# Two transformer blocks on one core: conditional passes announced to the instruction fetch, and attention values one step later

## The chip, the cores and the metric

The kernel runs on one core of a Trainium2 chip. The metric is the device time of one execution in microseconds (us); the figure of a kernel is the median of several executions. Engines are named as in the profile: PE (TensorE, matmuls), PEld (its weight loads), DVE (VectorE), ACT (ScalarE), POOL (GpSimd), SP (SyncE, which issues the weight transfers). "PEq" and "PEldq" are PE's sequencer: semaphore events, register loads and branches.

## What is computed

256 tokens of width 1024 go through two blocks in float32. Each block is a mixer with three branches and then a mixture of experts:

```python
def first_block(x, ...):
    h = rms_norm(x, norm_mix) * (1 + sc_m) + sh_m
    x = x + g_m * hybrid_mixer(h, ...)          # linear recurrence, two attentions
    h = rms_norm(x, norm_ffn) * (1 + sc_f) + sh_f
    return x + g_f * moe_ffn(h, ...)            # 32 experts, top 4, w1 1024x2048, w2 1024x1024

def second_block(x, mem, ...):
    y_ssm = s5_branch(u_ssm, ...)               # complex state space, scans along the sequence
    y_dsa = dsa_branch(q, k, v, ...)            # 8 heads, top 64 keys of each query
    y_mem = memory_branch(qm, km, vm)           # 4 heads over 256 memory rows
    merged = g_s * (y_ssm @ w_up_ssm) + g_d * (y_dsa @ w_up_dsa) + g_m * (y_mem @ w_up_mem)
    x = x + merged @ w_out
    return x + hier_moe(rms_norm(x), ...)       # 32 experts in 4 groups, top 2
```

## The kernel before, in words

Each engine has its own instruction stream, written out by hand in one order; they meet at semaphores. `Queue` (L65) wraps an engine with the semaphore it raises, so `t(ins)` marks an instruction and returns its number, and the tables `pe`, `act` and `dve` hold these marks for the others to wait on. The program is written twice, once dry to fill the tables.

**First mixture** (`tensor_moe1`, L824). The weights of expert u are six transfers of 2 MB, w1 in four and w2 in two, 192 in all, which SP issues in order into eight slots of `ring` (`fetcher`, L303; `sync`, L325). A slot is filled again when PE has passed the marks that free it. The rows of an expert are gathered in groups of 32, up to four passes. The first pass is always computed. The others lie in the code behind the first and run only when a register with the expert's row count says so. This happens in three places for each expert: after either half of layer one, and after layer two's first pass. In each place the code of passes two to four comes first, and the short part that stands for "not more than 32 rows" comes after it, so a small expert jumps forward over all of the code of passes two to four. In a pass one half of layer one has 16 matmuls (32 rows x 512 columns, plus four for the bias in half one), and so has all of layer two. The helpers are `only` (L737) and `either` (L745); the places are L929 (`either(t, x, count, 32, second)`, twice per expert) and L961 to L973 (the If of the second pass of layer two and its Else). In the trace L748 is the condition of `either`, L755 the event that its Else raises, L962 the condition of the second pass of layer two, L970 and L973 the events of its Else. After either half, PE goes on with `spread1` of the expert before (L835; in the trace matmuls of L481), with the gather of the next expert and with layer two. The core of `either` is:

```python
with t.e.If(count > limit):
    body()
with t.e.Else():
    t.e.wait_ge(x.sem, m)
    t.e.nop().then_inc(x.sem, x.n - m)
```

**Second attention** (`tensor_dense2`, L981; `scalar_dense2`, L2442; DVE's loop behind L2022). Twelve units u = 0 to 11 (0 to 3 memory heads, 4 to 11 sparse heads) go through a pipeline of steps s. Per step PE does `scores(s)` (L1046, or L1049 and L1053), `turn_p(s-2)` (L609, transposes of the weights, in the trace L613) and `values(s-2)` (L1062 or L1067), with half a gate projection (L596) between them in steps 0 to 2. DVE does the row maximum of s (L1534, L1536), the scaling of the weights of s-1 (L1547, L1549) and one step of the state-space scan of group 0 (L2012 in steps 2 to 9, of 256 columns; other lines of 1024 columns in the first two and last four steps). ACT copies the result of values(s-3) out (L2520 or L2523), copies the turned weights of s-2 out of PSUM (`scalar_turned_p`, L2255; in the trace L2259) and takes the exponentials of s (`scalar_exps`, L2242; in the trace L2247). The turned weights lie in `PT[u % 2]`, two buffers; their PSUM bank (lane 6) and that of the values (lane 7) are single; `scalar_turned_p` of u waits for PE's values of u-2. After the loop PE does `driven(1)` (L1027), the input of the scan of group 1, and DVE the scans of groups 1, 2 and 3 (`scans`, L2022), each followed by `states` on PE (L1081; in the trace L488). Transfers for what follows wait for PE's mark of the last values (`pv`, 2, 11).

**Second mixture** (L1138 onward): 96 transfers of 2 MB in ten slots, no branches.

Of the kernel before, what the change touches and what calls it, by code (L numbers as in the profile page):

```python
# [64 lines left out]
class Queue:  # L65

    def __init__(self, e, sem):
        self.e, self.sem, self.n, self.met = e, sem, 0, {}

    def wait_ge(self, sem, value):
        if self.met.get(id(sem), 0) < value:
# [39 lines left out]
def build(nc, a, out, ctx):  # L112
# [632 lines left out]
    def either(t, x, count, limit, body):  # L745
# [6 lines left out]
        with t.e.Else():  # L752
            if m > 0:
                t.e.wait_ge(x.sem, m)
            t.e.nop().then_inc(x.sem, x.n - m)  # L755

    def tensor_rows(t, w, tb):

        for g in range(2):
            b = w.claim("rows", 1, tb, g)  # L760
            for i in range(4):
                ins = t.e.transpose(b[:, TB(i)], HV[:, 4 * g + i, TB(tb)], ident)
            pe["rows", 1, tb, g] = t(ins)
# [60 lines left out]
    def tensor_moe1(t, w):  # L824
        e = t.e
        tensor_route(t, w, 1, WR1, 32, 128)
        gather_rows(t, w, 1, 0, TL1)
        gather_weights(t, w, 1, 0, TL1)
        tensor_ada(t, w, 5, 1)
        t.wait_ge(s_dve, dve["flag", 1])  # L830
        t.wait_ge(s_b1, 16)

        x, y, z = Queue(e, s_px), Queue(e, s_py), Queue(e, s_ps)

        def spread1(u, count):  # L835
            spread(t, w, 1, u, TL1)

            def second_half():
                t.wait_ge(s_act, act["yg", 1, u, 1])
                for tb in range(2):  # L840
                    for h in range(2):
                        b = w.claim("sp", 1, u, 1, tb, h, lane=TL1X)
                        psp[u, tb, h] = z(e.matmul(b[:, :], SWT[u % 2][:, 1, TB(tb)], YG_[1][:, HALF(h)], start=True,
                                                   stop=True))

            either(t, z, count, 64, second_half)
            psp["all", u] = z.n

        def biases():

            for h in range(2):
                tensor_ada_out(t, w, 5, h, TL1)
            b = w.claim("ct", lane=TL1)
            for tb in range(2):
                ins = e.transpose(b[0:32, TB(tb)], CMB[:, tb, :], ident)
            pe["ct"] = t(ins)
            t.wait_ge(s_dve, dve["ct"])
            t.wait_ge(s_b2, 16)
            for tb in range(2):
                for h in range(2):  # L860
                    b = w.claim("y0", tb, h, lane=TL1)
                    pe["y0", tb, h] = w.sums(b[:, :], [(CT[:, TB(tb)], B2[:, HALF(h)])])

        counts = [e.value_load(flag(0))]
        for u in range(NE):
            HG, AT_ = HGB[u % 2], ATB[u % 2]
            pick = ident[0:32, u:u + 1].to_broadcast([32, 32])
            t.wait_ge(s_act, act["hg", 1, u])

            def layer1(b, n, half, arrive):  # L870

                if half == 0:
                    for s in range(4):
                        e.matmul(b[32 * s:32 * s + 32, :], pick, B1R[:, HALF(s)], start=True, stop=False)  # L874
                for c in (2 * half, 2 * half + 1):
                    if arrive:
                        w.weights("w1", u, c)
                    W = RG_(slot["w1", u, c], 0, 2, 2048)
                    for r in range(2):
                        for s in range(4):  # L880
                            ins = e.matmul(b[32 * s:32 * s + 32, :], HG[:, 2 * c + r, 32 * n:32 * n + 32],  # L881
                                           W[:, r, HALF(s)], start=False, stop=(c == 3 and r == 1))
                return ins

            def layer2(b, n, arrive, first):

                for s in range(4):
                    if arrive and s % 2 == 0:
                        w.weights("w2", u, s // 2)
                    W = RG_(slot["w2", u, s // 2], 0, 2, 2, 1024)  # L890
                    for h in range(2):
                        for r in range(2):
                            ins = e.matmul(b[64 * h + 32 * r:64 * h + 32 * r + 32, :],  # L893
                                           AT_[:, 2 * s + r, 32 * n:32 * n + 32], W[:, s % 2, r, HALF(h)],
                                           start=(s == 0), stop=(s == 3))
                            if first is not None:
                                first(ins)
                                first = None
                return ins

            def turn_act(k, passes):
                b = w.claim("at", u, k, lane=TL1)
                t.wait_ge(s_dve, dve["ac", u, passes[-1]])
                for i, n in enumerate(passes):
                    for r in range(2):
                        ins = e.transpose(b[:, TB(2 * i + r)], ACB[:, n, TB(r)], ident)  # L906
                return ins

            count = counts[u]
            b0 = w.claim("l1", u, 0, lane=(0,))  # L910
            for half in range(2):
                pe["l1", u, half] = t(layer1(b0, 0, half, True))
                if half == 1 and u + 1 < NE:
                    counts.append(e.value_load(flag(u + 1)))

                def further(n):
                    if half == 0:
                        w.claim("l1", u, n, lane=(n,))
                    return layer1(ps("l1", u, n), n, half, False)

                def third():
                    only(t, count, 96, lambda: further(3))
                    further(2)

                def second():
                    only(t, count, 64, third)
                    x(further(1))

                either(t, x, count, 32, second)  # L929
                for c in (2 * half, 2 * half + 1):  # L930
                    w.free("w1", u, c)
                    px["free", "w1", u, c], py["free", "w1", u, c] = x.n, 0
            px["l1", u] = x.n
            if u > 0:
                spread1(u - 1, counts[u - 1])
            if u == LATE_BIAS:
                biases()
            pe["at", u, 0] = t(turn_act(0, (0,)))
            if u + 1 < NE:
                gather(t, w, 1, u + 1, TL1)  # L940
            turn_act(1, (1,))
            t.wait_ge(s_act, act["at", u, 0])

            def first_second(ins):
                pe["at", u, 1] = t(ins)

            def first_third(ins):
                px["at", u, 2] = x(ins)

            pe["l2", u, 0] = t(layer2(w.claim("l2", u, 0, lane=(7,)), 0, True, first_second))  # L950

            def fourth():
                layer2(w.claim("l2", u, 3, lane=(3,)), 3, False, None)

            def third():
                t.wait_ge(s_act, act["at", u, 2])
                only(t, count, 96, fourth)
                y(layer2(w.claim("l2", u, 2, lane=(2,)), 2, False, None))

            m, met = (x.n, y.n), dict(t.met)  # L961
            with e.If(count > 32):  # L962
                only(t, count, 64, lambda: turn_act(2, (2, 3)))
                t.wait_ge(s_act, act["at", u, 1])
                x(layer2(w.claim("l2", u, 1, lane=(1,)), 1, False, first_third))
                either(t, y, count, 64, third)
            t.met = met
            with e.Else():
                t.e.wait_ge(s_px, m[0])
                e.nop().then_inc(s_px, x.n - m[0])  # L970
                if m[1] > 0:
                    t.e.wait_ge(s_py, m[1])
                e.nop().then_inc(s_py, y.n - m[1])  # L973
            px["l2", u] = x.n
            py["l2", u] = y.n
            for g in range(2):
                w.free("w2", u, g)
                px["free", "w2", u, g], py["free", "w2", u, g] = x.n, y.n
        spread1(NE - 1, counts[NE - 1])

    def tensor_dense2(t, w):  # L981
# [86 lines left out]
                                       start=(c == 0), stop=(c == 1))  # L1068
            pe["pv", 2, u] = t(ins)

        for s in range(14):
            if s < 12:
                scores(s)
            if s >= 2:
                turn_p(t, w, 2, s - 2, (0, 1), 2)
            if s < 3:
                gate_half(t, w, 2, 11 + s)
            if s >= 2:
                values(s - 2)

        def states(c):  # L1081
            WR_, WM_, TA_, TB_ = W5[c % 2]
# [1359 lines left out]
    def scalar_dense2(s):  # L2442
# [84 lines left out]
            if u == 11:  # L2527
                act["branch", 2, 1] = k

        for k in range(14):  # L2530
            if k >= 3:
                values(k - 3)
            if k >= 2:
                scalar_turned_p(s, 2, k - 2, 4)
            if k < 12:
                scalar_exps(s, 2, k, 256, 128.0 ** -0.5 if k < 4 else 0.125, False)
# [170 lines left out]
```

## Time and profile before

| | us |
|---|---|
| median of 3 executions | 2187.61 |
| lowest and highest | 2186.37, 2188.66 |
| the profiled execution | 2187.02 |
| its span, first to last instruction | 2185.2 |
| PE busy | 1818.3 |
| DVE busy | 804.7 |
| ACT busy | 506.8 |
| read from HBM | 709.35 MB |

The span is what the rows further down are counted in (their times run from its start); the profiled execution's own time has 1.8 us more around it. PE's busy time is modelled and the matmuls overlap, so its share says little by itself: what counts is which wait ends last in each stretch.

### The profile page before, as it was taken

Reading aid. Unit: us, or ns where it says so; the run is one execution under the profiler, and the core shown is the slowest. Engines: PE = TensorE matmul, PEld = TensorE weight load, DVE = VectorE, ACT = ScalarE, POOL = GpSimd, SP = SyncE. Lnnn points to the kernel's source line nnn. Section 1 sums busy time; section 2 is a strip of 40 time slices with the busy share of each in tenths; the row PEclk is TensorE's granted clock in tenths of the full one; section 3 lists DMA queues with packets and bytes.
Section 4 is the critical chain, followed back from the end, with each engine's and each line's share of the span. In section 5 each row is a group of like instructions: output and inputs, shape, how many; then the busy total and the mean of one; then the engine's idle time right before and its main releaser. Section 6 shows DMA issues by size and latency. Waiting matters only on the chain. (4 is left out here: it accounts for less than half of the span.)

```text
span 2185.2 us, 28329 instructions
## 1 busy us (share of the span) xinstructions
PE 1818.3 (83%) x11496; PEld 826.7 (38%) x11496; DVE 804.7 (37%) x1613; ACT 506.8 (23%) x1028; POOL 77.5 (4%) x96
## 2 busy tenths in 40 slices
PE   7899998999999998989987797699889855665556
PEld 3655445433333433424333233255544522222221
DVE  2215533333342444434443334588782200000001
ACT  2022302232331233332333233222310200000000
POOL 0000000000000000000000000084000000000000
PEclk9999999999999999989999999799999878887888
DMA  7845359789897799999999999534128299999997
GB/s 281 287 136 191 136 173 388 314 350 409 343 420 312 309 424 423 423 422 399 425 423 423 422 423 423 180 121 178 54 101 345 87 429 427 427 428 428 427 429 322
DMA packets 114820, 713.55 MB, mean 327 GB/s; under 512 B 16799, under 2 KB 21102, under 8 KB 69006
## 3 DMA queue, kind: packets, MB, share of 16 engines
q1 hardware_dynamic: 106208, 704.98, 79.1%
q10 hardware_dynamic: 8398, 5.47, 0.8%
q8 instruction: 165, 2.70, 0.5%
q14 instruction: 49, 0.40, 0.0%
HBM read 709.35 MB, written 1.07 MB: 325 GB/s over the span
## 5 line engine op out<-in xcount | busy, mean ns | idle before, releaser
L881 PE MATMUL ps<-ring,ar 128*32 128x512 f32 x3072 | 371.9, 624 | 44.3 <-DMA ring<-in_w 31.6
L481 PE MATMUL ps<-ar 128*128 128x128 f32 (+5 forms) x1742 | 351.4, 359 | 38.3 <-PEq L755 16.4
L488 PE MATMUL ps<-ring,ar 128*32 128x512 f32 x1184 | 196.1, 692 | 139.0 <-DMA ring<-in_w_gate 49.2
L481 PEld LDWEIGHTS ps<-ar 128*128 128x128 f32 (+2 forms) x1742 | 233.9, 200 | 159.4 <-issue 114.3
L481 PE MATMUL ps<-ring,ar 128*128 128x512 f32 (+2 forms) x592 | 247.0, 577 | 4.9 <-ACT ar L2266 2.6
L881 PEld LDWEIGHTS ps<-ring,ar 128*32 128x32 f32 x3072 | 97.8, 113 | 314.3 <-issue 264.7
L1825 DVE TENSOR_SCALAR ar<-ps 128x256 f32<-128x256 f32 x128 | 54.4, 425 | 409.7 <-PE ps L881 400.9
L893 PE MATMUL ps<-ring,ar 128*32 128x512 f32 x1536 | 173.8, 598 | 0.0
L596 PE MATMUL ps<-ring,ar 128*128 128x512 f32 x384 | 171.9, 599 | 0.0
L481 PEld LDWEIGHTS ps<-ring,ar 128*128 128x128 f32 x592 | 112.4, 191 | 132.8 <-issue 126.2
L2400 ACT ACTIVATE ar<-ps 64x512 f32<-64x512 f32 x256 | 151.5, 592 | 45.1 <-PE ps L893 30.7
L1748 DVE TENSOR_TENSOR ar<-ps,ar 128x512 f32<-128x512 f32 x176 | 121.7, 692 | 91.0 <-PE ps L481 80.7
L488 PEld LDWEIGHTS ps<-ring,ar 128*32 128x32 f32 x1184 | 54.9, 124 | 247.5 <-issue 246.7
L488 PE MATMUL ps<-ar 128*32 128x512 f32 x288 | 112.6, 701 | 36.8 <-DMA ring<-in_w_up 21.3
L2389 ACT ACTIVATE ar<-ar 128x256 f32<-128x256 f32 x128 | 53.3, 416 | 322.0 <-DVE ar L1825 316.0
L1835 DVE TENSOR_TENSOR ar<-ar 128x256 f32<-128x256 f32 x128 | 79.6, 622 | 97.2 <-ACT ar L2389 90.4
L2437 ACT ACTIVATE ar<-ps 128x256 f32<-128x256 f32 x128 | 49.2, 384 | 252.3 <-PE ps L906 203.5
L596 PEld LDWEIGHTS ps<-ring,ar 128*128 128x128 f32 x384 | 71.8, 192 | 80.9 <-issue 80.5
L2124 DVE TENSOR_TENSOR ar<-ps,ar 128x512 f32<-128x512 f32 x8 | 5.5, 692 | 263.1 <-ACT ar L2576 263.1
L893 PEld LDWEIGHTS ps<-ring,ar 128*32 128x32 f32 x1536 | 46.3, 110 | 100.4 <-issue 100.4
L2368 ACT ACTIVATE ar<-ps 128x512 f32<-128x512 f32 x80 | 47.8, 597 | 95.1 <-PE ps L481 95.1
L874 PE MATMUL ps<-ar 32*32 32x512 f32 x384 | 54.1, 619 | 14.4 <-PEq L973 10.3
(403 smaller groups left out, 1379.0 us busy)
## 6 DMA issues: line engine op xcount, KB each, us to landing
ring<-in_w SPq DMA_DIRECT2D x192, 2048.0 KB, 20.4
ring<-in_w_gate SPq DMA_DIRECT2D x25, 2048.0 KB, 29.1
ring<-in_w_up SPq DMA_DIRECT2D x25, 2048.0 KB, 31.4
ring<-in_w_down SPq DMA_DIRECT2D x24, 2048.0 KB, 29.8
ring<-in_w_in SPq DMA_DIRECT2D x21, 2048.0 KB, 9.0
ring<-in_w_ada SPq DMA_DIRECT2D x12, 2048.0 KB, 8.3
ar<-in_w_up SPq DMA_DIRECT2D x7, 2048.0 KB, 29.8
ar<-in_w_gate SPq DMA_DIRECT2D x7, 2048.0 KB, 29.3
```

The lines of the kernel that those rows point to most:

```text
L481: ins = self.t.e.matmul(o, l, r, start=(i == 0), stop=(i == len(pairs) - 1))
L488: ins = self.t.e.matmul(b[32 * i:32 * i + 32, :], l, r, start=(k == 0), stop=(k == len(steps) - 1))
L596: ins = t.e.matmul(b[:, :], HV[:, k, TB(tb)], W[:, k, :], start=(k == 0), stop=(k == 7))
L874: e.matmul(b[32 * s:32 * s + 32, :], pick, B1R[:, HALF(s)], start=True, stop=False)
L881: ins = e.matmul(b[32 * s:32 * s + 32, :], HG[:, 2 * c + r, 32 * n:32 * n + 32], W[:, r, HALF(s)], start=False, stop=(c == 3 and r == 1))
L893: ins = e.matmul(b[64 * h + 32 * r:64 * h + 32 * r + 32, :], AT_[:, 2 * s + r, 32 * n:32 * n + 32], W[:, s % 2, r, HALF(h)], start=(s == 0 ...
L1748: k = v(v.own.tensor_tensor(o, b, o, ALU.add))
L1825: dve["glu", u, n] = v(v.own.tensor_scalar(glu, b[:, 0:512:2], 7.0, None, ALU.min))
L1835: dve["ac", u, n] = v(v.own.tensor_tensor(o, lin.rearrange("p (q r) -> p q r", r=2), sg.rearrange("p (q r) -> p q r", r=2), ALU.mult))
L2389: act["sg", u, n] = s(s.own.activation(M[:, 512:768], M[:, 0:256], ACT.Sigmoid, scale=1.702))
L2400: k = s(s.own.activation(YG_[n // 2][64 * (n % 2):64 * (n % 2) + 64, HALF(h)], ps("l2", u, n)[64 * h:64 * h + 64, :], ACT.Copy))
L2437: m = s(s.own.activation(o, ps("at", u, k)[:, 256 * i:256 * i + 256].rearrange("p (r s n) -> p r s n", r=2, s=4), ACT.Copy))
```

## The change

Three edits.

There are three hints per expert: before the first half of layer one, right after the first branch for the second, right after the second for the branch in layer two.
2. The three places are rewritten with a new function `announced`, which writes the compare-and-branch and the two parts by hand: the branch is taken to "other" when the count is below 33, the body follows it. The nested conditions (64 and 96 rows) stay as they were, without hints.
3. In the second attention, `values` on PE goes from step s-2 to step s-3, with one step more at the end, and its copy on ACT from k-3 to k-4. `turn_p` and the copy of the turned weights stay where they were.

```diff
+    def announced(t, name, count, limit, notice, body, other):
+
+        e, met = t.e, dict(t.met)
+        part = lambda end: e if t.dry else nc.body(f"{name}_{end}", valid_engines=[e.engine])
+        e.br_lt(count, limit + 1, on_true=f"{name}_other", on_false=f"{name}_body").branch_hint(notice)
+        with part("body"):
+            body()
+            e.br(f"{name}_end")
+        t.met = met
+        with part("other"):
+            other()
+            e.br(f"{name}_end")
+        if not t.dry:
+            nc.switch_bb(f"{name}_end")
...
             count = counts[u]
+            more = e.to_reg(count > 32)
+            notice = e.mark_branch_hint_location(more)
             b0 = w.claim("l1", u, 0, lane=(0,))
...
-                either(t, x, count, 32, second)
+                m = x.n
+
+                def none():
+                    if m > 0:
+                        e.wait_ge(s_px, m)
+                    e.nop().then_inc(s_px, x.n - m)
+
+                announced(t, f"first{u}_{half}", count, 32, notice, second, none)
+                notice = e.mark_branch_hint_location(more)
...
-            with e.If(count > 32):
+            def second_pass():
                 only(t, count, 64, lambda: turn_act(2, (2, 3)))
...
-            with e.Else():
-                t.e.wait_ge(s_px, m[0])
+            def no_second_pass():
+                e.wait_ge(s_px, m[0])
...
+            announced(t, f"second{u}", count, 32, notice, second_pass, no_second_pass)
...
-        for s in range(14):
+        for s in range(15):
             if s < 12:
                 scores(s)
-            if s >= 2:
+            if 2 <= s < 14:
                 turn_p(t, w, 2, s - 2, (0, 1), 2)
             if s < 3:
                 gate_half(t, w, 2, 11 + s)
-            if s >= 2:
-                values(s - 2)
+            if s >= 3:
+                values(s - 3)
...
-        for k in range(14):
-            if k >= 3:
-                values(k - 3)
-            if k >= 2:
+        for k in range(15):
+            if k >= 4:
+                values(k - 4)
+            if 2 <= k < 14:
                 scalar_turned_p(s, 2, k - 2, 4)
```

## Rows read from the trace of the kernel before

**Rows 1.** The page, its first line.

```profile
span 2185.2 us, 28329 instructions
```

**Rows 2.** Engines by stretch: busy us (count) of each, PEclk, DMA share, GB/s.

```profile
392.00:745.00 353.00, 335.48 (x2632) 128.90 (x2628) 126.43 (x264) 97.41 (x191) 0.00 (x0) 0.99 0.87 355
...
936.00:1380.00 444.00, 382.51 (x2738) 149.89 (x2734) 173.91 (x360) 140.87 (x275) 0.00 (x0) 0.95 1.00 417
...
1568.00:1628.00 60.00, 54.44 (x228) 24.70 (x224) 56.62 (x69) 4.27 (x6) 0.00 (x0) 0.96 0.25 88
...
1752.00:2172.00 420.00, 241.64 (x1706) 94.50 (x1702) 37.70 (x55) 28.38 (x50) 0.00 (x0) 0.79 1.00 425
```

**Rows 3.** The same view, one short stretch of the first mixture.

```profile
723.00:745.00 22.00, 20.63 (x182) 9.07 (x184) 8.53 (x19) 9.32 (x18) 0.00 (x0) 1.00 0.41 157
```

**Rows 4.** Waits of PE, 392 to 745 us: total us, times, longest.

```profile
PE ps L481 <- PEq L755: 5.4, 3, 2.5
...
PE ps L881 <- PEq L755: 1.2, 2, 1.0
```

**Rows 5.** Waits of PE, 936 to 1380 us.

```profile
PE ps L881 <- DMA ring<-in_w: 31.6, 16, 3.1
```

**Rows 6.** Timeline of PE, 421 to 432 us: start, us, what, idle before and releaser.

```profile
431.34 1.43 PE L481 MATMUL ps<-ar 128*128 128x512 f32 x2 [2.49 <-PEq L755]
```

**Rows 7.** Branches and Else events by line, 392 to 745 us: ns min/median/max, first and last.

```profile
L748 PEldq COMPARE_BRANCH  x55: 65/179/4721, 393.6 to 742.8; - x55
...
L962 PEldq COMPARE_BRANCH  x10: 70/76/422, 413.5 to 729.3; - x10
...
L973 PEldq EVENT_SEMAPHORE  x4: 51/51/51, 443.2 to 644.7; - x4
```

**Rows 8.** The same view of line 748 alone from 426.4 to 426.5 us, and of line 1202.

```profile
L748 PEldq COMPARE_BRANCH  x1: 4721/4721/4721, 426.5 to 426.5; - x1
...
L1202 PEldq COMPARE_BRANCH  x1: 3761/3761/3761, 1392.9 to 1392.9; - x1
```

**Rows 9.** Timeline of the second attention, one step with sparse heads.

```profile
1546.29 0.69 DVE L1534 TENSOR_REDUCE small<-ps 128x2 f32<-128x512 f32 x1 [0.90 <-PE ps L1053]
1546.73 0.60 ACT L2259 ACTIVATE ar<-ps 128x512 f32<-128x512 f32 x1 [1.34 <-PE ps L613]
...
1547.47 0.66 PE L1067 MATMUL ps<-ar 128*64 128x128 f32 x8 [0.78 <-ACT ar L2259]
...
1548.06 0.70 PE L1049 MATMUL ps<-ar 64*128 64x256 f32 x4
1548.27 0.69 DVE L2012 TENSOR_TENSOR_SCAN ring<-ar,ring 128x256 f32<-128x256 f32 x1
...
1548.69 1.13 PE L1053 MATMUL ps<-ar 128*128 128x256 f32 x4
...
1549.66 0.60 PE L613 MATMUL ps<-ar 128*128 128x128 f32 x4
1549.86 0.69 DVE L1534 TENSOR_REDUCE small<-ps 128x2 f32<-128x512 f32 x1 [0.90 <-PE ps L1053]
```

**Rows 10.** The same timeline, earlier steps, with memory heads' values, and one later scan step.

```profile
1528.66 1.05 PE L1062 MATMUL ps<-ar 128*128 128x128 f32 x8
1529.55 1.03 PE L1046 MATMUL ps<-ar 128*128 128x256 f32 x4
...
1538.69 0.69 DVE L1534 TENSOR_REDUCE small<-ps 128x2 f32<-128x512 f32 x1 [1.37 <-PE ps L1053]
...
1542.73 0.69 DVE L1534 TENSOR_REDUCE small<-ps 128x2 f32<-128x512 f32 x1 [1.37 <-PE ps L1053]
...
1558.97 1.23 DVE L2014 SCALAR_TENSOR_TENSOR ring<-ring 128x1024 f32<-128x1024 f32 x1
```

**Rows 11.** Waits of PE, 1528 to 1567 us.

```profile
PE ps L1067 <- ACT ar L2259: 6.3, 8, 0.8
```

**Rows 12.** Timeline behind the last scan: PE's first matmul after the wait.

```profile
1628.20 1.08 PE L488 MATMUL ps<-ar,ring 128*32 128x256 f32 x8 [4.97 <-DVE ring L2039]
```

More of the change, by code:

```diff
@@ L69, in __init__ @@
         self.e, self.sem, self.n, self.met = e, sem, 0, {}
+        self.dry = isinstance(e, Dry)
     def wait_ge(self, sem, value):
@@ L958, in third @@
                 y(layer2(w.claim("l2", u, 2, lane=(2,)), 2, False, None))
-            m, met = (x.n, y.n), dict(t.met)
-            with e.If(count > 32):
+            m = (x.n, y.n)
+            def second_pass():
                 only(t, count, 64, lambda: turn_act(2, (2, 3)))
@@ L966, in tensor_moe1 @@
                 either(t, y, count, 64, third)
-            t.met = met
-            with e.Else():
-                t.e.wait_ge(s_px, m[0])
+            def no_second_pass():
+                e.wait_ge(s_px, m[0])
                 e.nop().then_inc(s_px, x.n - m[0])
                 if m[1] > 0:
-                    t.e.wait_ge(s_py, m[1])
+                    e.wait_ge(s_py, m[1])
                 e.nop().then_inc(s_py, y.n - m[1])
+            announced(t, f"second{u}", count, 32, notice, second_pass, no_second_pass)
             px["l2", u] = x.n
```

## The prediction, made before the changed kernel was run

> **What bounds the kernel now.** I read the stages first, then PE's waits within the two stretches that the change touches, then the timeline of one step. The profiled execution took 2187.02 us around a span of 2185.2 us [rows 1]; that is 0.59 us below the median shown, 2187.61. All sums below are made against 2187.02.
>
> The first mixture has two regimes. From 392 to 745 us the weight transfers run at 355 GB/s with a DMA share of 0.87, from 936 to 1380 us at 417 GB/s with a share of 1.00 [rows 2]. In the first regime SP stands still in places because no ring slot is free: from 723 to 745 us the share is 0.41 at 157 GB/s, while PE is busy for 20.63 of 22 us [rows 3], and PE's waits there name no weight transfer, only small things, among them the Else event L755 [rows 4]. PE is the bound, and a microsecond that it loses or saves before 745 us moves all later transfers. In the second regime PE waits for weights, 31.6 us in 16 waits [rows 5]: transfers are the bound, and what PE saves there is waited away at the next transfer.
>
> In the second attention PE, ACT and PE again form one chain per step: PE turns the weights of u (L613), ACT copies them (L2259), and PE, which can do nothing else in its order, waits 0.78 us and then does the values (L1067) [rows 9]. From 1568 to 1628 us DVE's scans bound (56.62 of 60 us busy [rows 2]); PE waits for the last of them, 4.97 us [rows 12]. The second mixture runs at 425 GB/s with a share of 1.00 [rows 2]; it begins with its slots full, so that what the dense part saves ahead of it comes off the end in full.
>
> **The change, part by part. Values a step later.** PE's step with sparse heads starts its pieces at 1547.47 (values), 1548.06 and 1548.69 (scores) and 1549.66 (transposes) [rows 9]. Values cost 0.59 to the next start, scores 0.63 and 0.97; each is 0.07 to 0.16 shorter than the row's own duration, since matmuls overlap, so the transposes, 0.60, count for 0.44 by my estimate (the larger of the two cuts). That is 2.63 us of PE's own work in a period of 1549.86 - 1546.29 = 3.57 us [rows 9]; the other 0.94 is the wait for ACT and the drain around it. After the change the values that stand behind the transposes are those of the unit before, whose copy ACT has made a step ago, and the wait goes. Next in line is DVE: its row maximum starts at 1546.29 and its scan step ends at 1548.27 + 0.69 = 1548.96 [rows 9], 2.67 us of work; with a start I take 2.70 per step. ACT's share of a step is smaller (0.60 for the copy, then exponentials and the copy of the values), and all that it now does later it does in time that it idled, 1.34 us a step [rows 9].
>
> With the memory heads' values the period is 1542.73 - 1538.69 = 4.04 us [rows 10]; less 0.94 it is 3.10, PE's own. Step by step, taking DVE's row maximum of step s as the clock: the first values leave step 2, so step 3 starts 1529.55 - 1528.66 = 0.89 us earlier [rows 10]. Steps 4, 5 and 6 take 3.10 for 4.04: 2.82. Step 7 took 3.57 and now has the last memory values: 3.10, so 0.47. Steps 8, 9 and 10 take 2.70 for 3.57: 2.61. Before step 11 DVE has a scan step of 1.23 in place of 0.69 [rows 9, 10], so 3.24 for 3.57: 0.33. The sum is 7.1 us. Behind the last row maximum both kernels have the same chain (scaling, scan steps, last transposes, ACT's copy, last values): the values of unit 10 lie beside ACT's last copy. `driven(1)` and DVE's scans start 7.1 us earlier. Price range: the profile puts PE's waits for ACT under L1067 at 6.3 us in 8 times [rows 11], of which DVE keeps some back, so at least 4; at most, if DVE's idle time went entirely, 0.90 for each of eight steps [rows 9] and 0.89, 8.1. The buffers hold: ACT writes a `PT` buffer after the values of u-2, which stand one step ahead of it in PE's order, so this adds no wait. What follows is bound by DVE and then by PE; its transfers are issued at the marks that move with it, and the DMA share in that stretch is 0.25 [rows 2].
>
> **Announced conditions.** What there is to win is in the branches. Of the 55 executions of L748 before 745 us the median is 179 ns and the longest 4721; the ten of L962 stay below 422 ns [rows 7]. A long one empties PE's queue: the branch at 426.5 us took 4.72 us [rows 8], and PE stood 2.49 us [rows 6]; the other 2.23 us were covered by matmuls queued already. Before 745 us such idle time adds up to 5.4 + 1.2 = 6.6 us in five waits [rows 4]; this is all that hints can give, since what is lost later is covered by waiting for transfers [rows 5]. I take 0. Most taken branches are short: four experts with at most 32 rows end before 745 us [rows 7], and none of their L962 branches took over 422 ns, though each jumps over three passes. So the target normally is at hand, and a long branch must be one that comes too soon after the fetch had last moved on. 
>
> The Trainium skill's page Runtime: NRT & Kernel Launch, section Instruction fetch mechanics, says that instructions come in blocks of 256, that only the next block is fetched ahead, and that a taken branch stalls if its target is in neither. By that rule no jump of 240 reaches beyond the next block, a hint has nothing to redirect, and yet 4.72 us should not occur; the trace disagrees on the last point, so it must be lateness of the next block. By the rule the sum is that of 0; if the hints cured every stall of the rows it would be 6.6 lower.
>
> The hints and the register cost some five short sequencer instructions per expert. A branch that finds its target costs 65 to 76 ns [rows 7], so I bound each by 0.1 us; PE works off its queue meanwhile (2.23 us of cover above), so 0. Without cover it would be 0.5 us for each of ten experts before 745 us, 5 us. They also shift all later code, so that other branches come too soon; which ones I can't tell from rows, and take the number as unchanged, from none (6.6 saved) to twice as many (6.6 lost).
>
> The sum: 2187.02 - 7.1 - 0 = 2179.9 us. I predict 2180.0.
>
> **The rivals.** *Hints cure the stalls.* If the fetch starts on the target when the hint executes, 80 instructions or a whole half ahead, the lateness is gone. For it: the stalls are of the size of a fetch made at need, as at L1202, 3.76 us [rows 8]. Against it: the target already is next. Time: 2187.0 - 7.1 - 6.6 = 2173.3.
>
> *Hints misdirect the fetch; the kernel becomes slower.* If a hint makes the fetch leave out the block that comes next, or fetch one that is there, each announced branch of a small expert, or the code just behind it, waits. Place: 14 announced and taken branches before 745 us (four experts with three, one with two). Price: 2.49 us each [rows 6], 34.9, less the 6.6 there are: 28.3 more, 2187.0 - 7.1 + 28.3 = 2208. It decides over the sign from 7.1 us on, half a microsecond per branch. For it: nothing in this profile; against it: a hint at 1 does nothing, and one at 0 names a block that is wanted.
>
> *Another engine takes over in the attention.* If ACT's queue (the copy of the values now comes ahead of the copy of the weights) or DVE's holds the step at 3.1 or 3.2 us, the gain is 3 to 4 us: 2183.5.
>
> *The stalls only move.* The shift alone makes more branches late, 3 to 6 us more: 2183 to 2186.
>
> **How the numbers follow.** Forecast 0.55; cure 0.20; misdirection 0.09; another engine 0.08; moved stalls 0.08. A measurement of this kernel tells about 0.2%, 4.4 us, from no change. Faster by more: forecast, cure and a third of the two small ones, 0.80. Within: 0.12. Slower: misdirection less its mild cases, 0.08. The range holds forecast and cure and reaches into the moved stalls: 2172.5 to 2184.5.
>
> **What would show it.** Right: the row maxima L1534 of steps 8 to 10 stand 2.70 us apart, PE has no wait for L2259 at L1067, DVE's idle before L1534 is near zero there; from L1534 of step 11 to the end of the span the distance is unchanged; PEq waits at L755 and its successor before 745 us sum to 3 to 10 us. Wrong: they vanish (cure), or long branches stand at nearly every small expert (misdirection). Also wrong: DVE's scans from 1560 us on don't start earlier, or the second mixture's transfers wait for something else.

## The result, and the profile after

The changed kernel takes 2198.14 us (median of six executions, 2192.04 to 2199.65); beside it the kernel before took 2187.43 (six, 2185.67 to 2190.69). The ratio is 1.0037, 95% interval 1.0024 to 1.005: it is slower, by about 8 us by the ratio and 10.7 between the two medians, where 7 us less had been forecast; the stated range ended at 2184.5. The profiled execution took 2198.91 us, 11.9 more than the one before. (One of the twelve executions of `values_again` further down took 3727.53 us, in the slow state, and is left out of its figures.)

The two halves of the change went opposite ways. Take DVE's first sum behind the first mixture (L1854 before, L1883 after) as the border: it starts at 1399.83 us before and at 1418.90 after, 19.1 us later; from there to the end of the span are 785.4 us before and 778.2 after, 7.2 less. So the loss lies in the first mixture.

The page of the kernel after (its first line), and its engines by stretch, with the columns of [rows 2]:

```profile
span 2197.1 us, 28459 instructions
```
```profile
392.00:745.00 353.00, 331.07 (x2634) 129.79 (x2636) 126.67 (x264) 96.42 (x188) 0.00 (x0) 0.99 0.86 352
745.00:936.00 191.00, 166.35 (x1138) 69.24 (x1134) 78.84 (x161) 61.58 (x120) 0.00 (x0) 0.92 0.98 410
936.00:1380.00 444.00, 387.59 (x2770) 159.34 (x2766) 179.94 (x374) 143.68 (x281) 0.00 (x0) 0.94 0.98 408
```

The middle stretch before had 423 GB/s; in the last, transfers ran at 417 GB/s before [rows 2] and run at 408 now. Worked out from these rates (the difference times the length of the stretch), the transfers fell behind by some 3, 6 and 10 us in the three stretches: an estimate, but it accounts for nearly all of the 19.1 us and puts all but 3 of it behind 745 us, where the forecast had counted on cover. The transfers no longer bound in the last stretch, as PE's waits between 936 and 1380 us show (total us, times, longest):

```profile
PE ps L922 <- PEq L756: 11.1, 2, 5.6
PE ps L890 <- ACT ar L2466: 11.0, 4, 2.9
PE ps L897 <- issue: 9.4, 4, 3.3
PE ps L482 <- PEq L952: 8.9, 7, 2.4
PE ps L897 <- PEq L952: 5.3, 2, 3.1
PE ps L890 <- issue: 3.2, 1, 3.2
PE ps L897 <- DMA ring<-in_w: 2.1, 2, 1.9
```

The 31.6 us of waiting for weights [rows 5] have shrunk to 2.1, and waits for PE's own sequencer stand in their place. L952 is the event behind the announced conditions of layer one, L756 that behind the condition "more than 64 rows" of `spread1`, which is not announced (its branch is L749); what comes late is the branch ahead of them. The four waits put down to ACT's L2466 each follow an announced branch of layer two that took 4.7 to 5.1 us, so they belong here too. All but the last line sum to 48.9 us; in the kernel before, the same view has 19.8 us of such waits (7.6, 5.3, 4.6, 2.0 and 0.3). The growth, 29.1, is about what the wait for weights lost, 29.5. One trace does not fix the 19.8, though: with the mixture's code as it was before, the traces of `values_only` and `values_again` have 29.3 and 34.0 us of such waits there, and 22.2 and 26.8 of waiting for weights. The new and largest item is that of L756, two waits of over 5 us that the kernel before did not have.

Before 745 us the same view answers to [rows 4]:

```profile
PE ps L482 <- PEq L952: 4.1, 3, 2.6
PE ps L859 <- issue: 2.7, 1, 2.7
PE ps L890 <- ACT ar L2466: 2.3, 1, 2.3
PE ps L897 <- issue: 1.7, 1, 1.7
PE ps L890 <- issue: 1.5, 1, 1.5
PE ps L897 <- PEq L952: 1.0, 1, 1.0
```

Idle time for the events of announced branches is 5.1 us where it was 6.6: little was cured. But "issue", idle time without a releaser, is 5.9 us where it was 2.0, and the line with ACT is again a late branch, 4.53 us at 593.7 us.

In the second attention the clock of the steps, DVE's row maximum (L1563, before L1534), answers to [rows 9] and [rows 10]:

```profile
1563.94 0.69 DVE L1563 TENSOR_REDUCE small<-ps 128x2 f32<-128x512 f32 x1
1565.92 0.69 DVE L2041 TENSOR_TENSOR_SCAN ring<-ar,ring 128x256 f32<-128x256 f32 x1
1566.72 0.69 DVE L1563 TENSOR_REDUCE small<-ps 128x2 f32<-128x512 f32 x1
...
1569.49 0.69 DVE L1563 TENSOR_REDUCE small<-ps 128x2 f32<-128x512 f32 x1
...
1572.80 0.69 DVE L1563 TENSOR_REDUCE small<-ps 128x2 f32<-128x512 f32 x1
```

The steps are 2.78, 2.77 and 3.31 us; the brackets with idle time before them are gone, so DVE is the bound of these three steps. PE's waits from 1547 to 1586 us are now these, with no wait for the copy of the weights [rows 11]:

```profile
PE ps L614 <- DVE ar L1578: 2.8, 2, 1.8
PE ps L1096 <- ACT ar L2552: 0.4, 1, 0.4
```

### The profile page after: what moved, and what is told of

The parts are those of the page before. It is cut to its first block and busy times, and to the rows that moved or that the text cites. A ratio compares the mean times of both kernels' runs of the same rounds, so it can differ in the third digit from the quotient of the medians.

```text
span 2197.1 us, 28459 instructions
## 1 busy us (share of the span) xinstructions
PE 1823.7 (83%) x11496; PEld 836.6 (38%) x11496; DVE 804.9 (37%) x1613; ACT 507.2 (23%) x1028; POOL 77.5 (4%) x96
## 5 line engine op out<-in xcount | busy, mean ns | idle before, releaser
L482 PE MATMUL ps<-ar 128*128 128x128 f32 (+5 forms) x1742 | 355.6, 362 | 37.7 <-PEq L952 17.0
L482 PEld LDWEIGHTS ps<-ar 128*128 128x128 f32 (+2 forms) x1742 | 237.9, 203 | 157.1 <-issue 112.2
L482 PE MATMUL ps<-ring,ar 128*128 128x512 f32 (+2 forms) x592 | 247.0, 577 | 3.8 <-DVE ar L1452 1.9
L1854 DVE TENSOR_SCALAR ar<-ps 128x256 f32<-128x256 f32 x128 | 54.4, 425 | 406.0 <-PE ps L897 397.1
L482 PEld LDWEIGHTS ps<-ring,ar 128*128 128x128 f32 x592 | 112.4, 191 | 131.9 <-issue 126.2
L2466 ACT ACTIVATE ar<-ps 128x256 f32<-128x256 f32 x128 | 49.2, 384 | 270.1 <-PE ps L922 219.8
```

The costliest lines, as they stand in the source:

```text
L482: ins = self.t.e.matmul(o, l, r, start=(i == 0), stop=(i == len(pairs) - 1))
L1854: dve["glu", u, n] = v(v.own.tensor_scalar(glu, b[:, 0:512:2], 7.0, None, ALU.min))
L2466: m = s(s.own.activation(o, ps("at", u, k)[:, 256 * i:256 * i + 256].rearrange("p (r s n) -> p r s n", r=2, s=4), ACT.Copy))
```

## The experiments

Two theories stood after reading the two traces. Shift: the four added instructions per expert (one for the register, three hints) move all branches in the code, and more of them come before their block is fetched. Hint: announcing a branch that will be taken spoils the fetch in certain places. The Trainium skill's page Runtime: NRT & Kernel Launch, section Instruction fetch mechanics, says that code comes in blocks of 256 instructions, 16 KiB, and that only the next one is fetched ahead. The trace agrees on the size: queue 8, whose packets follow PE's branches and so carry PE's code, moved 2.70 MB in 165 packets, 16 KB each. "Fetch" below is the start of such a packet.

```profile
q8 instruction: 165, 2.70, 0.5%
```

### The two parts alone

`values_only` and `values_again` are the same kernel, the one before with the third edit alone; `announced_only` is the one before with edits 1 and 2.

> Only the attention edit; the first mixture is as before. If the attention gives what the two profiles suggest (DVE's first scan behind the attention starts 4.6 to 5.5 us earlier, seen from the end of the mixture, and the rest is 2.6 us shorter), the time is 2187.4 - 7.2 = 2180.2; if only the 4.6 us count, 2182.8. Rival: the two edits work on each other, and the attention alone gives nothing: 2187.

> The attention edit alone once more, beside far_early on one chip: five kernels that share it and differ in the mixture's code alone stood at 2183 to 2184.6, this one at 2179.7. If the layout of the branches costs those 3 to 5 us: 2179 to 2181 again. If that was chance: 2182 to 2184.

> Only the announced conditions; the attention is as before. If the parts add up: after plus what the attention gives, 2198.1 + 7.2 = 2205.3, and the mixture's end stands 19 us behind that of before. If the loss comes from something that both edits make together: less than 2200.

The attention alone gave 2179.74 us (ratio to before 0.9958, 0.9943 to 0.9974) and, run again, 2183.38 (0.9971, 0.9957 to 0.9984): 6 to 9 us less by the ratios, as forecast. The second figure is where its expectation put chance, not a cost of the layout, as the reason why other kernels stood 3 to 5 us above the first. The conditions alone gave 2203.5 (1.0079, 1.0064 to 1.0094): 15 to 17 us more. The parts add up, 1.0079 - 0.0036 = 1.0043 against the 1.0037 measured.

### The same code positions without hints, and with hints that say "straight on"

`shift_four` has the old branches and, in place of the four new instructions, empty events; `straight` is the changed kernel with a register that is always 1.

```diff
+            for _ in range(2):
+                e.nop().then_inc(s_pad, 1)
...
                 either(t, x, count, 32, second)
+                e.nop().then_inc(s_pad, 1)
```
```diff
-            more = e.to_reg(count > 32)
+            more = e.to_reg(count > -1)
```

> Values later, the old branches, no hints, but four empty events of PE per expert at the places of the register instruction and the three hints, so that every block of 256 instructions holds what it holds in the changed kernel. Shift theory (the loss comes from where branches fall in the blocks): 2197 to 2200, with the long branches at the same places as in the changed kernel, except those that need a hint. Hint theory (the loss is the hints' own): 2180 to 2182. If both have a share, in between: two stalls of 6.5 us at L749 in the changed kernel, both in same-block jumps, should be gone.

> The changed kernel, but the hinted register is always 1, so that each hint says that the branch goes straight on, wrongly for small experts. Shift theory: a hint that says straight asks only for what is fetched anyway, so the time is that of the shift alone, 2197 to 2200. Theory that a taken hint with its target in the same block puts off the next block: the two stalls of 6.5 us at L749 go, 5 us or so less than after: 2192 to 2194. Theory that the hint helps at long jumps: slower than after, over 2200.

They took 2184.62 us (0.9989, 0.9976 to 1.0003) and 2183.8 (0.9986, 0.9973 to 0.9999). The shift theory as the main cause has fallen: with the same number of instructions in the same places the time stays below that of the changed kernel, by 10 to 11 us by the ratios and 14 by the medians. So has the thought that hint instructions cost much in themselves: they are all executed in `straight`. What costs is a hint that says "taken". Both times also lie above the 2180 to 2182 of the pure hint theory, so that the shift may have a share. In `straight` the two waits for L756 are gone and the waits for weights are back; PE from 936 to 1380 us:

```profile
PE ps L897 <- DMA ring<-in_w: 21.8, 11, 3.0
PE ps L890 <- ACT ar L2466: 12.0, 4, 3.3
PE ps L482 <- PEq L952: 6.4, 5, 1.8
PE ps L897 <- PEq L952: 4.4, 2, 3.1
PE ps L897 <- issue: 4.3, 2, 2.9
```

Behind the first line these are 27.1 us (28.2 with one more of 1.1 us), inside the 19.8 to 34.0 of the three traces with the old code; the 48.9 of after stands out.

### Which hints

Laying the code of the changed kernel beside its trace gives the position of each executed branch. 63 announced branches are taken (21 experts with at most 32 rows, three each). At five the target lies in the same block as the branch, by my estimate of where blocks begin; there the branch takes 0.23 us, and the next fetch comes late: 8.5, 10.9 and 10.6 us after it at the second halves of experts 3, 16 and 22, where `straight` has 3.8, 3.6 and 3.5, and 4.5 and 4.3 us at layer two of experts 19 and 25, where `straight` has 2.3 and 2.7. The 40 others up to expert 23's second half take what they take in `straight`, within 0.7 us. Behind that, nine of the 18 others differ by 1.1 to 4.3 us, some longer and some shorter; why was not followed, so there the two kernels are not alike in all but the five. The first of the five is expert 3's second half. Timeline of PE after:

```profile
508.06 1.88 PE L859 MATMUL ps<-ar 128*128 128x512 f32 x4
510.28 0.70 PE L859 MATMUL ps<-ar 128*128 128x512 f32 x1 [0.34 <-DVE ar L1777]
513.63 2.08 PE L859 MATMUL ps<-ar 128*128 128x512 f32 x2 [2.65 <-issue]
```

and in `straight`:

```profile
511.25 1.98 PE L859 MATMUL ps<-ar 128*128 128x512 f32 x4 [0.34 <-DVE ar L1777]
```

PE runs into the end of its code within one group of four matmuls. The next fetch starts 8.5 us after the branch there (511.14 against 502.66), in `straight` 3.8 us after it (507.41 against 503.62). The clock makes it worse in this trace. Engines by stretch after, with PEclk as the third column from the right:

```profile
506.00:510.00 4.00, 3.75 (x9) 1.14 (x7) 3.48 (x6) 0.00 (x0) 0.00 (x0) 1.00 1.05 446
510.00:513.00 3.00, 0.70 (x1) 0.19 (x1) 0.92 (x2) 0.00 (x0) 0.00 (x0) 0.91 1.00 415
514.00:518.00 4.00, 4.00 (x11) 2.34 (x11) 1.95 (x4) 0.51 (x2) 0.00 (x0) 0.50 1.01 424
518.00:522.00 4.00, 4.00 (x32) 3.98 (x30) 1.15 (x3) 1.49 (x3) 0.00 (x0) 0.84 1.00 420
```

and in `announced_only`, which has the same stall (2.4 us):

```profile
514.00:518.00 4.00, 4.00 (x32) 3.47 (x32) 2.66 (x5) 1.58 (x3) 0.00 (x0) 1.00 0.95 395
```

Behind the idle 2.65 us the granted clock is 0.50, the lower level of 1.2 GHz, for some 5 us. Two of the four matmuls take 2.08 us, where in `straight` all four take 1.98. From expert 3's second branch to expert 4's first the changed kernel needs 25.5 us, `announced_only` 22.4 and `straight` 19.8. So the late fetch cost 2.6 us here, and the dip of the clock 3.0 more; the same stall can come with it or without. The same distance at experts 16 and 22 is 25.6 and 25.3 us after, 19.1 and 18.7 in `straight`. Not all of this stays: counted from expert 0's first branch, the changed kernel is 24.1 us behind `straight` at expert 23's first and 16.3 behind at expert 31's second.

Two kernels test this, each with the changed kernel's positions. `hint_across` leaves out the five hints, `hint_within` has only these five (empty events in the places of the others).

```diff
+    SAME = {(3, 1), (16, 1), (22, 1), (19, 2), (25, 2)}
...
+            def hint(k):
+                if (u, k) not in SAME:
+                    return e.mark_branch_hint_location(more)
+                e.nop().then_inc(s_pad, 1)
```

> The changed kernel, but five of its 96 branches go without a hint (an empty event stands in place of the hint instruction): expert 3, 16 and 22 at the second half of layer one, expert 19 and 25 at layer two. By the spacing of the code fetches these are the taken branches whose target lies in the same block of 256 instructions as the branch itself. Theory that only such hints cost: the time of the kernel with four empty events, 2183 to 2186, and PE's stalls of 6.5 us at L749 are gone. Theory that every hint of a taken branch costs a little: near 2195. Theory that hints across a block boundary help: below 2180.

> The complement: only those five branches have a hint, the other 91 have an empty event in its place; every block holds what it holds in the changed kernel. Theory that only such hints cost: the time of the changed kernel, 2196 to 2200. Theory that the loss is spread over all hints: near 2184.

91 hints: 2184.13 us (0.9982, 0.9967 to 0.9997), as without any. Five hints: 2197.0 (1.0035, 1.002 to 1.0051), the time of the changed kernel. So these five are what makes it slower than the layouts beside it. The waits of `hint_across` from 936 to 1380 us, and then those of `hint_within`:

```profile
PE ps L901 <- DMA ring<-in_w: 23.6, 12, 3.1
```
```profile
PE ps L926 <- PEq L756: 10.2, 2, 5.2
...
PE ps L901 <- DMA ring<-in_w: 5.7, 3, 3.0
```

The transfer queues in the 8 us behind expert 3's second branch, in `hint_across` (499.8 to 507.9 us) and in `hint_within` (500.4 to 508.6), show the fetch that is missing; packets, MB, share:

```profile
q1 hardware_dynamic: 235, 3.46, 100.6%
q8 instruction: 1, 0.02, 0.7%
```
```profile
q1 hardware_dynamic: 235, 3.46, 99.0%
```

### Another place for all of the code

> Values later and the old branches, no hints; one never taken body of 200 empty events stands ahead of expert 0, so that all code of the mixture lies 201 instructions further on. Nothing else changes. Shift theory: a block is late when PE passes the one before it in less than 5.9 us; worked out for this layout from the times of the branches, stalls before 745 us grow by 7 us (sum 14.6 against 7.7) and those of the whole mixture by 10: 2187 to 2190. Theory that the place of the code doesn't matter: 2179.7 to 2180.5.

> The changed kernel with all its hints, and a never taken body of 60 events ahead of expert 0: all its branches lie 61 instructions further on, nothing else differs. Theory that a taken hint within one block of 256 stops the fetch of the next block: the five stalls of the changed kernel (experts 3, 16 and 22 at half two, 19 and 25 at layer two) go, and late fetches stand at 14 to 16 other branches, among them half two of experts 5, 10, 11, 17, 23, 24, 29 and 30 and layer two of experts 1, 7, 13, 15 and 26. At the 2.6 us that each of the five cost (hint_within against hint_across, 12.9 us), 14 to 16 of them cost 36 to 42, less what is hidden: 2205 to 2225. Rival, that only the number of hints or their instructions count, or something peculiar to those five experts: 2184 to 2200.

The padding is a body behind a condition that is never true, ahead of expert 0:

```diff
         counts = [e.value_load(flag(0))]
+        with e.If(counts[0] > 4096):
+            for _ in range(60):
+                e.nop().then_inc(s_pad, 1)
```

`pad_200` took 2183.8 us (0.9985, 0.997 to 1.0). That is some 4 us above `values_only` and 0.4 above `values_again`, between the ranges of both theories, and my working of the late blocks failed: before 745 us PE waited 1.1 us for L755, less than the 6.6 of [rows 4], not more. `after_pad_60` took 2205.76 (1.0065, 1.0041 to 1.009), with a median in the range expected of the hint theory; but its five executions go from 2194.09 to 2206.29, two of them in or near the rival's range. What tells the theories apart is the trace. The late fetches at the five old places are gone (their branches now take 0.6 to 5.0 us, as jumps into the next block do) and new ones are there: at expert 5's second half the announced branch is short, as a jump within a block is, and PE stands later without a releaser. L762 and the timeline of PE there:

```profile
L762 PEldq COMPARE_BRANCH  x1: 233/233/233, 575.5 to 575.5; - x1
```
```profile
583.12 1.99 PE L859 MATMUL ps<-ar 128*128 128x512 f32 x4 [0.34 <-DVE ar L1780]
589.94 0.44 PE L925 MATMUL ps<-ar 128*128 128x128 f32 x2 [4.84 <-issue]
```

The next fetch came 12 us after that branch, and 8.3, 9.8 and 8.1 us after those of experts 11, 24 and 30. But only six branches were of this kind, not 14 to 16: these four and layer two of experts 15 and 21 (0.24 and 0.23 us, next fetch 4.3 and 4.2 us later). The others that the expectation names took 3.2 to 5.0 us, so they did leave their block, and my block boundaries are off there. Five of the six are among those it names. At 2.6 us each, six come to 16 us, not to 36 to 42, so that the median fell into the range is partly luck. The branches behind new block starts have a share that is not known (six announced first halves take 6.0 to 6.5 us here); no kernel with this layout and without hints was run.

### Hints for a jump that is far

Behind the mixture PE, DVE and ACT branch over a region of thousands of instructions (L1202). PE's 3.76 us there [rows 8] hurt nobody, but DVE's stand on the chain that ended last. These kernels have the attention edit, the old branches in the mixture, and a hint for this one on PE and DVE.

```diff
-            self.cond = q.e.If(q.e.value_load(flag) > 0)
+                q.e.br_lt(value, 1, on_true=self.end, on_false=f"{name}_body").branch_hint(notice)
...
+            value = q.e.value_load(FLG[m - 1][0:1, 0:1].bitcast(I32))
+            notices[q.e.engine, m] = value, q.e.mark_branch_hint_location(q.e.to_reg(value > 0))
```

> Values later and the old branches, without hints in the mixture; but the branch of L1202 behind the mixture, which skips a region of thousands of instructions, is announced on PE and on DVE ahead of the last expert's spread. In the trace with the attention edit alone, PE's branch there takes 3.48 us and DVE stands 3.50 us behind its own, on the chain that ended last. Theory that a hint starts the fetch of its target: both shrink below 0.5 us and the time falls by 3.0, 2179.7 to 2176.7. Theory that a hint only stops the fetch of the next block: the same stall or a longer one, 2179.7 to 2183.

> As far_hint, but the hint for the far branch behind the mixture executes much earlier: on PE at the start of the last expert (some 900 instructions ahead), on DVE three experts ahead. In far_hint it executed 8.3 us ahead of PE's branch, but after PE had entered the block that holds the branch; PE still took 3.23 us there and DVE 2.80 us behind its own. Theory that the choice of the next block to fetch falls on entering a block, and that a hint turns it to the target: both branches fall below 0.6 us, DVE's chain is 2.8 us shorter, 2180 to 2177. Theory that hints do nothing at far targets either: the same 3 us on both, 2180 to 2184.

> far_early with a never taken body of 28 events ahead of expert 0, so that the mixture's code lies 29 instructions further on; the sum of late blocks worked out from the branch times would fall from 42 to 35 us over the whole mixture, but the same working failed for the shift by 201. If the layout is worth 3 to 5 us either way: between 2174 and 2182; if it is worth nothing that can be measured: as far_early.

With the hint late (`far_hint`: 2183.03 us, 0.9969, 0.9953 to 0.9985) both stalls stayed, 3.23 us on PE and 2.80 behind DVE's branch. With the hint early both went. The two kernels load and compare the value alike and differ only in when that and the hint execute: 8.2 us ahead of PE's branch in `far_hint`, 36.5 in `far_early`. That it is the entry into the block that decides, and not the time ahead, no run separates. DVE's first sum in `values_again`, then the same in `far_early`; the last line is PE's branch in `far_early`:

```profile
1403.61 1.23 DVE L1854 TENSOR_TENSOR ar<-ar 128x1024 f32<-128x1024 f32 x1 [3.36 <-issue]
```
```profile
1393.04 1.23 DVE L1880 TENSOR_TENSOR ar<-ar 128x1024 f32<-128x1024 f32 x1 [0.73 <-DVEq L1797]
...
L1210 PEldq COMPARE_BRANCH  x1: 444/444/444, 1388.5 to 1388.5; - x1
```

`far_early` took 2180.22 us (0.9976, 0.9962 to 0.9989) and `far_early_28` 2182.04 (0.9973, 0.996 to 0.9986). The stall fell by 2.6 us in the trace, but it did not come off the end. From DVE's first sum to the end of the span are 781.7 us in `far_early` and in `far_early_28`, 779.1 in `values_again`, 779.6 in `far_hint`. The difference lies behind the attention: from DVE's row maximum of step 11 to PE's first matmul behind the last scan are 70.2 us in these two and 67.9 in `values_again` and `far_hint`, and in these two the clock is 0.50 for 5 us around the start of `driven(1)`. Such a dip stands in `values_only` too, which has no hint, so that the early hint brings it on is not shown. These two, `far_hint` and the attention edit alone are faster than the kernel before by 0.2 to 0.4% and can't be told from each other.

## Why the prediction was wrong

**The term that failed** is the "- 0" for the announced conditions, a sum of nothing with bounds of 6.6 us either way. `announced_only` measured it at 15 to 17 us more. Two steps behind it were wrong, the second decisively.

**What bounds, and the cover behind 745 us.** The two regimes were read rightly, but the step "what is lost later is covered by waiting for transfers" failed. The cover was finite, 31.6 us [rows 5], and its use is in the rows: 2.1 us of it are left. The stretch was never summed. From 936 to 1380 us the waits for the sequencer went from 19.8 us (29.3 and 34.0 in the other two traces of that code) to 48.9, which used up what there was to hide, and four of the five harmful hints lie at 935.9 us or behind.

**Hints at 0.** This is the step that decided the sign. "A hint that names the target doesn't start that fetch earlier if it is already the next one due" held for the 58 branches whose target lies in the next block: together they cost nothing that can be told, 0.9982 in `hint_across` against 0.9989 and 0.9986 in `shift_four` and `straight`. It didn't ask about a target in the branch's own block. Its own numbers held the case: a jump of 192 instructions inside blocks of 256 stays in its block from up to a quarter of all positions (an estimate; three of the 21 second halves did, four in `after_pad_60`). In the five cases of this kind a fetch that would have been made was made late: `hint_within` against `hint_across` is 2197.0 - 2184.1 = 12.9 us (11.6 by the ratios), 2.6 per case on average, net of what later waits give back and with the lower clock in it. The rival "hints misdirect the fetch" had this mechanism, "make the fetch leave out the block that comes next", and got 0.09; its place and size were wrong. It charged 14 branches before 745 us (13 by the trace: expert 10's second stands at 746.6), where one of the five lies; all five, four of them where it had seen no cost, come to 13 us, not 28.

**Hints cure the stalls** is refuted: long announced branches stayed, the longest 6.37 us. Where a hint did cure (`far_early`), the target was far and the hint came early.

**The hint instructions** were bounded at 0.1 us each; they take 0.03 to 0.05 us, and `straight` shows that they cost nothing that can be told.

**The shift.** `shift_four`, `straight`, `hint_across` and `pad_200` (two layouts) stand at 0.9982 to 0.9989, the two runs of `values_only` at 0.9958 and 0.9971. The difference of means is 0.2%, 4 us, inside the forecast's plus or minus 6.6, but the intervals of 0.9971 and of all four overlap, so that the shift cost anything is not shown. A visible piece are two branches, of experts 14 and 15, which by my positions lie 13 and 23 instructions behind the start of a block: 6.06 and 6.37 us in the changed kernel, 5.96 and 5.86 in `shift_four`, which has no hints, 1.43 and 1.61 in `values_again`. The 4 us themselves rest on runs that scatter by 10 us, and the working for `pad_200` failed.

**Values later** was right in nearly every term, after against forecast: the first values leave step 2, 0.90 (0.89); the three steps with memory values 3.02, 3.31 and 3.02 (3.10 each); the fourth 3.02 (3.10); three steps of 2.77 (2.70); the last 3.31 (3.24). From the first row maximum to the last 44.17 us became 37.34, 6.8 less against 7.1. One thing behind it was not forecast: with the edit PE waits for DVE ahead of the last transposes (1.8 and 1.1 us), and in some kernels, the changed one among them, the clock then falls. From 1577 to 1582 us it is 0.54, and `driven(1)` (L482) takes 2.11 us for 1.17; DVE's work on the scan of group 1 starts 4.6 us earlier, counted from the border, not 7.1. In `values_again`, with the same two waits, the clock stays up and it starts 6.3 us earlier. "From L1534 of step 11 to the end of the span the distance is unchanged" came out in the number, 624.6 us before and 624.3 after, by two things that cancel: 2.2 us more to PE's first matmul behind the last scan, and 2.6 us less from there to the end (557.0 and 554.4), mostly PE's matmuls under L482 from 1693.81 us, which take 20.87 us at a clock of 1.00 where they took 22.56 at 0.95. `values_again` has 557.1 there, so this is the clock of one execution and not the edit, and that the whole came to 7.2 us is partly luck.

## What to carry to other kernels

In these runs a branch hint did something useful only where the target lay beyond the block that would be fetched next and the hint executed early, and even there the time did not show it. For the shorter jumps it did nothing or harm, and which ones it harmed depended on where the code happened to lie, so an edit elsewhere moved the damage. When a stretch is "covered" by waits, sum the cover and compare it with the sum of what may be lost there.

## What the runs showed of the hardware

- Behind an announced taken branch within its block (0.23 to 0.25 us) the next fetch comes late: 8 to 12 us behind the branch at the second half, instead of 3.5 to 4.0 without that hint, and PE stands 2.3 to 5.6 us; at layer two 3.9 to 4.6 us instead of 2.3 to 2.7.
- A branch that came too early ended 2.5 us after the start of the fetch that it waited for (first branch of expert 14: fetch 3.58 us behind its start, end at 6.06; expert 24's at layer two: 2.59 and 5.07).
- A hint for a far jump 36.5 us ahead took PE's branch from 3.71 to 0.44 us (and, three experts ahead, DVE's gap from 3.36 to 0.73); 8.2 us ahead it left 3.23 us. In the second case PE had entered the branch's block about 1 us before the hint, by an estimate from the next fetch, which started 2.4 us behind it.
- Idle time of 2.65 us on PE was followed by about 5 us at a granted clock of 0.50; in `hint_within` by a shorter dip, 0.68 and 0.89 in two stretches of 4 us; in `announced_only` by none. So the same stall costs a different amount from execution to execution.
- A branch that by my positions is 13 or 23 instructions behind the start of a block, with its target in the next, takes 5.9 to 6.4 us with a hint or without.
